# Weight products that read their moving tile alternately from two halves

## The reference

```python
def _swiglu(h, w_gate, w_up, w_down):
    return (jax.nn.silu(h @ w_gate) * (h @ w_up)) @ w_down

...
        h = _rms_norm(x, ffn_norm[l])
        x = x + _swiglu(h, w_gate[l], w_up[l], w_down[l])
...
    mod = c_act @ ada_w[l] + ada_b[l]
    sh1, sc1, g1, sh2, sc2, g2 = jnp.split(mod, N_MOD, axis=-1)
    h = rms_norm(x, mix_pre_g[l]) * (1.0 + sc1[:, None, :]) + sh1[:, None, :]
    y = hybrid_mixer(h, w_in[l], conv_w[l], conv_b[l], conv_ln_g[l], conv_ln_b[l], w_out[l])
    x = x + g1[:, None, :] * rms_norm(y, mix_post_g[l])
    h = rms_norm(x, ffn_pre_g[l]) * (1.0 + sc2[:, None, :]) + sh2[:, None, :]
    y = swiglu_ffn(h, w_gate[l], w_up[l], w_down[l])
    x = x + g2[:, None, :] * rms_norm(y, ffn_post_g[l])
```

## Time and profile before

| | |
|---|---|
| median of 3 runs | 2215.75 us (2215.17 to 2216.69) |
| profiled execution, span from first to last instruction | 2213.5 us (2.25 us below the median; no other time is shown for it) |
| TensorE busy | 2190.3 us, 99% |
| VectorE busy | 1602.6 us, 72% |
| ScalarE busy | 1097.1 us, 50% |
| granted TensorE clock, mean | 0.999 of full speed |
| DMA | 526.46 MB, mean 238 GB/s |

### The profile page before, as it was taken

One profiled execution on the slowest core, in us unless ns is written; L12 is line 12 of the kernel. 1 busy time (PEld: TensorE's weight loads), 2 busy tenths in 40 slices (PEclk: granted clock), 3 DMA queues, 4 the chain that ended last, 5 costly groups with the idle time before them and its releaser, 6 DMA issues.

```text
span 2213.5 us, 29238 instructions
## 1 busy us (share of the span) xinstructions
PE 2190.3 (99%) x9949; PEld 1812.7 (82%) x9949; DVE 1602.6 (72%) x2077; ACT 1097.1 (50%) x1537; POOL 236.2 (11%) x215
## 2 busy tenths in 40 slices
PE   9999999999999999999999999999999999999998
PEld 7888888888888888888888887788888888888886
DVE  7656688888787878778866898897887455554555
ACT  6555574544434444344455776654444444434444
POOL 5004000000000000000002886000010000000000
PEclk9999999999999999999999999999999999999999
DMA  8776629899988998899746674768997677766764
GB/s 284 210 211 190 196 73 326 270 298 299 295 291 288 301 307 286 293 290 306 266 146 202 191 212 145 270 227 257 305 299 245 194 201 203 204 191 191 201 203 146
DMA packets 376233, 526.46 MB, mean 238 GB/s; under 512 B 120856, under 2 KB 129432, under 8 KB 375856
## 3 DMA queue, kind: packets, MB, share of 16 engines
q1 hardware_dynamic: 375536, 523.87, 76.0%
q10 hardware_dynamic: 576, 1.05, 0.2%
HBM read 510.15 MB, written 2.10 MB: 231 GB/s over the span
## 4 chain that ended last, share of the span: by engine, by line
PE 92%; DVE 3%; ACT 2%; DMA 1%; issue 1%; POOL 1%; SPq 0%; DVEq 0%; ACTq 0%; POOLq 0%
PE bank L1181 31%; PE bank L1197 29%; PE bank L1198 29%; DVE w_both L2250 1%; DMA raw<-in_w_in 1%; POOL convT L969 1%; PE bank L1252 1%; PE bank L1285 0%; PE bank L1273 0%; PE bank L1320 0%; ACT w_both L1671 0%; ACT zsb L1612 0%; DMA x_t<-in_x_t 0%; PE bank L1071 0%; PE bank L1166 0%
## 5 line engine op out<-in xcount | busy, mean ns | idle before, releaser
L2250 DVE TENSOR_TENSOR w_both<-raw,w_both 128x1024 fp32r<-128x1024 f32 x762 | 945.9, 1246 | 508.5 <-ACT w_both L1671 499.5
L1671 ACT ACTIVATE w_both<-raw 128x1024 fp32r<-128x1024 f32 x762 | 805.5, 1060 | 991.0 <-PE bank L1181 914.0
L1197 PE MATMUL bank<-w_both,act_hi 128*128 128x512 f32 x1984 | 774.2, 390 | 0.0
L1198 PE MATMUL bank<-w_both,act_lo 128*128 128x512 f32 x1984 | 772.2, 389 | 0.0
L1181 PE MATMUL bank<-w_both,act_hi 128*128 128x512 f32 x2160 | 576.1, 390 | 0.8 <-issue 0.5
L1181 PEld LDWEIGHTS bank<-w_both,act_hi 128*128 128x128 f32 x2160 | 404.1, 188 | 86.1 <-DVE w_both L2250 1.5
L1197 PEld LDWEIGHTS bank<-w_both,act_hi 128*128 128x128 f32 x1984 | 372.5, 188 | 76.8 <-issue 0.2
L1198 PEld LDWEIGHTS bank<-w_both,act_lo 128*128 128x128 f32 x1984 | 372.5, 188 | 76.6
L1197 PE MATMUL bank<-w_both,mid_hi 128*128 128x512 f32 x960 | 376.0, 392 | 3.9 <-DVE mid_lo L2382 2.4
L1198 PE MATMUL bank<-w_both,mid_lo 128*128 128x512 f32 x960 | 373.7, 389 | 0.0
L2208 DVE SCALAR_TENSOR_TENSOR ada_acc<-ada_raw,c_act,ada_acc 128x512 f32<-128x512 f32 x360 | 269.8, 749 | 11.5 <-DMA ada_raw<-in_ada_w 4.4
(11 more groups left out here) (319 smaller groups left out, 1010.6 us busy)
## 6 DMA issues: line engine op xcount, KB each, us to landing
ada_raw<-in_ada_w SPq DMA_DIRECT2D x192, 512.0 KB, 5.4
raw<-in_w_gate SPq DMA_DIRECT2D x176, 512.0 KB, 4.6
raw<-in_w_up SPq DMA_DIRECT2D x176, 512.0 KB, 4.9
raw<-in_w_down SPq DMA_DIRECT2D x176, 512.0 KB, 4.5
raw<-in_w_in SPq DMA_DIRECT2D x166, 512.0 KB, 4.4
raw<-in_w_out SPq DMA_DIRECT2D x60, 512.0 KB, 5.4
h_tok<-h_blk SPq DMA_DIRECT2D x256, 32.0 KB, 4.3
x_res<-in_x SPq DMA_DIRECT2D x8, 256.0 KB, 5.7
```

The source lines that it names most:

```text
L1197: pe.matmul(A_[t][:, :], h_, w_hi[:, s, kk, :], start=(k == 0), stop=False)
L1198: pe.matmul(A_[t][:, :], l_, w_hi[:, s, kk, :], start=False, stop=False)
L1671: act.activation(w_hi[:, U % SPLIT_SLOTS].rearrange("p k n -> p (k n)"), raw_of(c, u).rearrange("p k n -> p (k n)"), ACT.Copy).then_inc(hi ...
L2250: dve.tensor_tensor(w_lo[:, U % SPLIT_SLOTS].rearrange("p k n -> p (k n)"), raw_of(c, u).rearrange("p k n -> p (k n)"), w_hi[:, U % SPLIT_ ...
```

## The change

Four small helpers give views of a tile. `by_half` sees a tile of 512 columns as two halves of 256; `apart` sees it as its even columns and then its odd ones; `in_turn` walks the two halves alternately, one element of each; `pairs` walks a bank in its usual order, written with the same two dimensions. The two splits now read raw weights with a step of two elements and write the even columns to the first half of `w_hi` or `w_lo`, the odd ones to the second. Every weight product reads its moving tile with `in_turn`, which restores the old order of columns, so the banks hold what they held. The chunks of the compressed keys and values keep the old forms. No instruction is added or taken away, and none stands elsewhere on its engine.

```diff
+        def in_turn(tile):
+
+            return tile.rearrange("p (a b) -> p b a", a=2)
+
+        def pairs(bank_):
+
+            return bank_[:, :].rearrange("p (b a) -> p b a", a=2)
+
+        def apart(tile):
+
+            return tile.rearrange("p k (b a) -> p k a b", a=2)
+
+        def by_half(tile):
+
+            return tile.rearrange("p k (a b) -> p k a b", a=2)
...
-                            ins = pe.matmul(A_[t][:, :], a[:, k, t * P:(t + 1) * P], w[:, s, kk, :],
+                            ins = pe.matmul(pairs(A_[t]), a[:, k, t * P:(t + 1) * P], in_turn(w[:, s, kk, :]),
...
-                        pe.matmul(A_[t][:, :], h_, w_hi[:, s, kk, :], start=(k == 0), stop=False)
-                        pe.matmul(A_[t][:, :], l_, w_hi[:, s, kk, :], start=False, stop=False)
+                        pe.matmul(pairs(A_[t]), h_, in_turn(w_hi[:, s, kk, :]), start=(k == 0), stop=False)
+                        pe.matmul(pairs(A_[t]), l_, in_turn(w_hi[:, s, kk, :]), start=False, stop=False)
...
-                    act.activation(w_hi[:, U % SPLIT_SLOTS].rearrange("p k n -> p (k n)"),
-                                   raw_of(c, u).rearrange("p k n -> p (k n)"), ACT.Copy).then_inc(hi_done, 1)
+                    if c["C"] is None:
...
+                    else:
+                        act.activation(by_half(w_hi[:, U % SPLIT_SLOTS]), apart(raw_of(c, u)), ACT.Copy).then_inc(hi_done, 1)
...
-                    dve.tensor_tensor(w_lo[:, U % SPLIT_SLOTS].rearrange("p k n -> p (k n)"),
-                                      raw_of(c, u).rearrange("p k n -> p (k n)"),
-                                      w_hi[:, U % SPLIT_SLOTS].bitcast(F32).rearrange("p k n -> p (k n)"),
-                                      ALU.subtract).then_inc(lo_done, 1)
+                    if c["C"] is None:
...
+                    else:
+                        dve.tensor_tensor(by_half(w_lo[:, U % SPLIT_SLOTS]), apart(raw_of(c, u)),
+                                          by_half(w_hi[:, U % SPLIT_SLOTS].bitcast(F32)), ALU.subtract).then_inc(lo_done, 1)
```

More of the change, by code:

```diff
@@ L1032, in early_gemm @@
                         for t in range(TT):
-                            ins = pe.matmul(A_[t][:, :], a[:, k, t * P:(t + 1) * P], w[:, u, kk, :],
+                            ins = pe.matmul(pairs(A_[t]), a[:, k, t * P:(t + 1) * P], in_turn(w[:, u, kk, :]),
                                             start=(k == 0 and a is act_hi and w is w_hi), stop=False)
@@ L1494, in first_units @@
                     act.wait_ge(raw_half[u] if kk == 0 else raw_loaded[u], 16)
-                    ins = act.activation(w_hi[:, u, kk, :], raw[:, u, kk, :], ACT.Copy)
+                    ins = act.activation(by_half(w_hi[:, u, kk:kk + 1, :]), apart(raw[:, u, kk:kk + 1, :]), ACT.Copy)
                     ins.then_inc(half_hi if kk == 0 else hi_done, 1)
@@ L1670, in split @@
                         act.wait_ge(parts_used, at(U - SPLIT_SLOTS + 1, r, 2 * c["nu"]))
-                    act.activation(w_hi[:, U % SPLIT_SLOTS].rearrange("p k n -> p (k n)"),
-                                   raw_of(c, u).rearrange("p k n -> p (k n)"), ACT.Copy).then_inc(hi_done, 1)
+                    if c["C"] is None:
+                        act.activation(w_hi[:, U % SPLIT_SLOTS].rearrange("p k n -> p (k n)"),
+                                       raw_of(c, u).rearrange("p k n -> p (k n)"), ACT.Copy).then_inc(hi_done, 1)
+                    else:
+                        act.activation(by_half(w_hi[:, U % SPLIT_SLOTS]), apart(raw_of(c, u)), ACT.Copy).then_inc(hi_done, 1)
                     after(u)
@@ L1940, in first_units @@
                         dve.wait_ge(hi_done, u + 1)
-                    dve.tensor_tensor(w_lo[:, u, kk, :], raw[:, u, kk, :], w_hi[:, u, kk, :].bitcast(F32),
+                    dve.tensor_tensor(by_half(w_lo[:, u, kk:kk + 1, :]), apart(raw[:, u, kk:kk + 1, :]),
+                                      by_half(w_hi[:, u, kk:kk + 1, :].bitcast(F32)),
                                       ALU.subtract).then_inc(half_lo if kk == 0 else lo_done, 1)
@@ L2249, in split @@
                         dve.wait_ge(parts_used, at(U - SPLIT_SLOTS + 1, r, 2 * nu))
-                    dve.tensor_tensor(w_lo[:, U % SPLIT_SLOTS].rearrange("p k n -> p (k n)"),
-                                      raw_of(c, u).rearrange("p k n -> p (k n)"),
-                                      w_hi[:, U % SPLIT_SLOTS].bitcast(F32).rearrange("p k n -> p (k n)"),
-                                      ALU.subtract).then_inc(lo_done, 1)
+                    if c["C"] is None:
+                        dve.tensor_tensor(w_lo[:, U % SPLIT_SLOTS].rearrange("p k n -> p (k n)"),
+                                          raw_of(c, u).rearrange("p k n -> p (k n)"),
+                                          w_hi[:, U % SPLIT_SLOTS].bitcast(F32).rearrange("p k n -> p (k n)"),
+                                          ALU.subtract).then_inc(lo_done, 1)
+                    else:
+                        dve.tensor_tensor(by_half(w_lo[:, U % SPLIT_SLOTS]), apart(raw_of(c, u)),
+                                          by_half(w_hi[:, U % SPLIT_SLOTS].bitcast(F32)), ALU.subtract).then_inc(lo_done, 1)
                     after(u)
```

## The result

The changed kernel takes 2177.56 us (2175.5 to 2178.86, 4 runs) against 2215.67 of the kernel before (its three runs and one more): a ratio of 0.983, with a 95% interval of 0.981 to 0.984. It is faster by 38 us, or 1.7%, where 8290 us was forecast.

The account below looks back on a forecast made before the run. TensorE's weight products, 9120 at 227.5 ns, were taken as the bound; 2215.75 us plus 6069 for their far reads plus 0 for the splits and the rest gave 8285, stated as 8290 us, range 3600 to 8500.

Parts of the forecast that it names:

- What bounds the kernel: TensorE's 9120 weight products at 227.5 ns, 2075 of 2213.5 us; each nanosecond added to one product costs 9.12 us.
- The forecast's floor: Lower bound for alternating reads in the products: 0 ns added, since 512 columns at 2.4 GHz are 213 ns.
- Step (1): Products' alternating reads of the moving tile: 1.744 ns a column, 665.5 ns more a product, 6069 us more in all.
- Step (2): ScalarE's copies and VectorE's subtractions reading raw with a step of two: taken as 0, VectorE at most +0.72 us a unit.
- F: Nothing changes, 2216 us: columns fetched far enough ahead, or by two readers for even and odd columns; chance 0.13.
- G: Products get faster because alternating halves relieve crowded neighbouring reads: at most 128 us less, 2090 us; chance 0.03.
- A: In the products each far column costs its own block, 1.744 ns: 8290 us; chance 0.38.
- B to D: Product reads: half rate, 4290 us (0.25); VectorE's additional time carries over, 5510 us (0.12); its ratio carries over, 3630 us (0.05).
- B: Product reads at half rate, a single costing as much as a pair: 455 ns a product, 4290 us; chance 0.25.
- E: TensorE reads freely but the splits pay the far price, 8% in some stretches: near 2300 us; chance 0.04.

Follow-up runs that it names:

- the read alone: Kernel before with only the products changed to read in turn from two halves, splits plain: 2127.27 us, ratio 0.960.
- step_four_read: Kernel before with products reading every fourth column, in four passes (a step of 16 bytes): 4344.97 us, ratio 1.960.
- splits_only: Changed kernel with the products put back to reading 512 neighbouring columns, splits still stepped: 2216.91 us, ratio 1.000.
- The two one-sided runs: Changed kernel with one split plain again: VectorE's plain, 2135.32 us, ratio 0.963; ScalarE's plain, 2161.78 us, ratio 0.975.
- near_in_turn: Kernel before with products reading single columns in turn from two neighbouring blocks of four: 2127.13 us, ratio 0.960.
- halves_by_two: Kernel before with products reading singly from two halves in turn, every second column first, the rest in a second pass: 2216.24 us, ratio 1.000.

## Why the prediction was wrong

**What bounds the kernel** was right. A nanosecond a product is worth 9.12 us: the read alone took 11.5 ns off and 88 us of the possible 105. Of the other 17, seven are idle time of TensorE, 30 us instead of 23; its busy time fell by 95 and not by 105 us. About half of those ten are the clock, by an estimate from its mean (0.996 of 2125 us against 0.999 of 2214). The rest lies within the error of a pace read from eight steps to 0.01 us, about 1 ns or 9 us. The forecast's floor, that a product "can't easily be below", was also crossed, as the pace fell from 227.5 to 216 ns.

**Step (1), the price of a far read, failed**, at "So both engines look as if a block of four neighbours (16 bytes) came in about 1.75 ns, whether one or four of its elements are used". On VectorE one price for two far steps may be right. The step to TensorE rested on two matching numbers: 1.77 ns per four neighbours on TensorE, 1.744 ns per far element on VectorE. step_four_read is the fair test, for there no two successive columns share a block: 460 / 512 = 0.90 ns a column, half of the 1.744. And the changed kernel's pattern isn't of that kind: it takes all four columns of each block within eight reads, alternately from two blocks, where the forecast charged each column as if it opened a block anew. Measured for term (1): -11.5 ns a product, not +665.5. The rule of the Trainium skill that the prediction drew on (SBUF — State Buffer, the section on the DMA port swizzle), that each access to a new line pays, fails on this pattern too, and the measurement decides: the changed kernel's read crosses to another block at every column and is the fastest here (216 ns). Crossing at every column doesn't tell the pace by itself, since other reads that do so took 227 (halves by two), 282 (quarters) and 460 ns (step of four). Nor are two columns of a block in succession enough: the step of two has them and takes 452 ns.

The following table sets the seven paces against what each of two readers meets. "Opens" counts the blocks of four that one reader goes to anew, in each four of its own reads; a step is the time in which each reader takes one column, 216 / 256 = 0.84 ns, and the extra steps are pace / 216 x 4 - 4.

| order of reading | one reader's reads | opens in 4 | pace, ns | extra steps in 4 |
|---|---|---|---|---|
| halves singly; near blocks singly | a0 a1 a2 a3 | 1 | 216 | 0 |
| neighbours; halves by two | a0 a2, a4 a6 | 2, never one after another | 227 | 0.2 |
| fours in turn | a0 a2, b0 b2 | 2, never one after another | 250 | 0.6 |
| quarters singly | a0 c0 a1 c1 a2 c2 a3 c3 | 1, two after another | 282 | 1.2 |
| pairs in turn | a0 b0 a2 b2 | 2, one after another | 333 | 2.2 |
| step of two | 0, 4, 8, 12 | 4 | 452 | 4.4 |
| step of four | 0, 8, 16, 24 | 4 | 460 | 4.5 |

If two blocks stay open for each reader, an opening costs about one step when it comes right after or before another (1.1 in the last three rows, 1.2 for quarters), and little when other reads lie between. That there are two readers and not one is argued from halves by two: one reader would open four blocks in eight columns there and two with neighbours, yet both take 227 ns. That a block is four columns is argued too: with blocks of two, neighbours would open at every read as the step of two does (227 against 452), and with blocks of eight a step of four would open twice as often as a step of two (460 against 452). Two of the rows, halves by two and step of four, were forecast from it. The rest was fitted afterwards. What it doesn't explain is fours in turn, 23 ns above neighbours though its readers open as often, and why quarters cost 1.2 and not 1.0. The readers themselves aren't seen in any trace; another mechanism that counts in the same way would do. That stays open.

**Step (2), the splits, was half wrong.** "I take 0" holds with the products as they were (splits_only: VectorE 1245 ns, ScalarE +73). The change has both parts, and the splits then take 1582 and 1545 ns. The prediction asked what hides a slow split, but never whether TensorE's new read would slow it. Its upper bound of +0.72 us a unit for VectorE held (+0.30). The worry was the right one, in "While TensorE keeps today's pace that would matter": with a unit at 12 x 216 ns = 2.59 us VectorE is busy 94% of the stretch from 420 to 900 us. The two one-sided runs put 8 and 35 us on the splits, 43 of the 50 us between 2127.27 and 2177.56. Between the profiles of those two, TensorE has 37 us more idle time and 15 more busy time. Some 11 of the 15 are the clock, an estimate from its mean (0.991 of 2177 us against 0.996 of 2125): a wait costs more than its own length where the clock falls behind it.

**Rivals.** F named two readers, each of which finds neighbours, "which is just what the halves give them", and gave that 0.13 with no change; the readers fit, and F failed only in that neighbours as they were read before left room. G had the sign: "the 14 ns by which a product exceeds 213". Of the 14, 11.5 came. Its reason, that neighbouring reads crowd one place and distance relieves them, isn't borne out: near_in_turn gains as much with blocks side by side, and halves_by_two gains nothing with columns 1024 bytes apart. Its chance of 0.03 was too small: the excess of 14 ns, in the same rows that served to argue for A, said that contiguous reads had something to lose. B to D fell with A. B's 455 ns is nearly what the step of two (452) and the step of four (460) cost, but not what the change does. E had slow splits, but at another price and without the gain of the reads.

## What to carry to other kernels

When products of fp32r are the bound, read their pace from the starts and compare it with 512 columns at the granted clock: here 227 ns against 213, and alternate reading from two blocks of 16 bytes took off 11.5 of the 14 ns between them. Put the columns right while emptying the bank, where a step of two cost nothing, and not in the splits, where it made two engines slow beside TensorE's reads in turn. A far read priced on VectorE did not give TensorE's price; and an untried access pattern deserves one run with the pattern alone before it is priced.

## What the runs showed of the hardware

- The pace of the same product ranged from 216 to 460 ns by the order of its reads alone, and singles from two halves were faster than neighbours. Pairs from the same halves took 333 ns.
- Bank writes in jumps of pairs cost nothing that could be measured (2216.51 us against 2216.13), and neither did bank reads with a step of two by VectorE (682 ns against 683) and ScalarE (585 and 585).
- Engines slow each other without a wait between them. With products in turn, a step of two on either side of a split made ScalarE's 1566 to 1594 ns and VectorE's 1545 to 1631. In the run with VectorE's step GpSimd slowed as well, its conv additions from 1116 to 1297 ns, and in the changed kernel to 1309; with ScalarE's step alone they took 1133. Why is open.
- Behind waits of TensorE the granted clock fell. In the changed kernel TensorE was busy 3.68 of 6.5 us, and right behind that the granted clock was 0.68 in the mean of 10 us, a mix of the full level (2.4 GHz) and the half (1.2 GHz), where the kernel before, busy throughout, kept 1.00 from 1050 to 1065 us. The mean over the span is 0.991, before it was 0.999:

```profile
1048.00:1054.50 6.50, 3.68 (x20) 3.02 (x20) 6.33 (x8) 4.01 (x5) 0.00 (x0) 1.00 0.77 249
1055.00:1065.00 10.00, 9.47 (x31) 7.83 (x32) 6.45 (x8) 2.61 (x3) 0.00 (x0) 0.68 0.93 337
```
